# A two-layer S5/FNet backbone in split fp32r: seams between sections run in two halves of the tokens, with three PSUM slots

## What is computed

```python
def _pre(x, g, mod, k):
    return _rmsnorm(x, g) * (1.0 + mod[:, 3 * k + 1][:, None]) + mod[:, 3 * k][:, None]
def _post(x, y, g, mod, k, weight):
    return x + weight * mod[:, 3 * k + 2][:, None] * _rmsnorm(y, g)
...
for l in range(DEPTH):
    x = _post(x, _swiglu(_pre(x, g[0], mod_lat, 0), ffn1_gu[l], ffn1_down[l]), g[1], mod_lat, 0, 0.5)
    h = _pre(x, g[2], mod_lat, 1) @ w_in[l]
    y = jnp.concatenate([_s5_mixer(...), _fnet(...)], axis=-1) @ w_out[l]
    x = _post(x, y, g[3], mod_lat, 1, 1.0)
    x = _post(x, _swiglu(_pre(x, g[4], mod_lat, 2), ffn2_gu[l], ffn2_down[l]), g[5], mod_lat, 2, 0.5)
```

## Time and profile before

| what | us |
|---|---|
| runs of the program: median (lowest to highest) | 2869.12 (2868.15 to 2871.7) |
| the profiled execution: its time | 2866.32 |
| the profiled execution: its span in the trace | 2864.4 |
| PE busy | 2680.7 (94%) |
| DVE busy | 1677.3 (59%) |
| POOL busy | 821.0 (29%) |
| ACT busy | 716.3 (25%) |

### The profile page before, as it was taken

The page is one execution under the profiler, slowest core; times in us unless marked ns, Lnnn a source line. Parts: engine busy times, 40 slices in busy tenths (PEclk is TensorE's granted clock), DMA queues, the critical chain, the costliest instruction groups (busy, mean ns, idle before and its releaser), DMA issues.

```text
span 2864.4 us, 39514 instructions
## 1 busy us (share of the span) xinstructions
PE 2680.7 (94%) x16446; PEld 2496.0 (87%) x16446; DVE 1677.3 (59%) x2235; ACT 716.3 (25%) x977; POOL 821.0 (29%) x1292
## 2 busy tenths in 40 slices
PE   5899999998899889999999799999998898899996
PEld 4899999997869789999999699999998766588885
DVE  5868877865582686766665743343434683644444
ACT  4211121113413421111111322112122413322222
POOL 1258775732050200000000228767551050100001
PEclk9999999999999999999999899999999999899998
DMA  9443444442455134343441232222233455133321
GB/s 314 125 132 125 152 152 128 129 165 87 151 147 162 45 111 125 111 130 114 132 126 52 74 74 87 95 94 89 94 103 120 138 167 161 57 96 99 96 89 59
DMA packets 340459, 337.09 MB, mean 118 GB/s; under 512 B 52529, under 2 KB 311225, under 8 KB 336697
## 3 DMA queue, kind: packets, MB, share of 16 engines
q1 hardware_dynamic: 279224, 204.07, 24.3%
q10 hardware_dynamic: 51840, 77.07, 8.0%
q0 software_dynamic: 9216, 53.42, 5.0%
...
...
## 4 chain that ended last, share of the span: by engine, by line
PE 81%; DVE 11%; ACT 3%; DMA 2%; issue 2%; SPq 1%; POOL 0%; DVEq 0%; ACTq 0%; POOLq 0%
PE ps L454 71%; DVE adaW L541 3%; PE ps L1390 2%; PE ps L582 2%; PE ps L1089 2%; ACT wH L439 1%; PE ps L1415 1%; DVE tmpN L1168 1%; DMA y_d<-YC 1%; DVE wL L446 1%; DVE rmsX L1177 1%; DVE xT L1049 1%; PE ps L1404 1%; DMA xin<-in_x_dram 1%; PE ps L1074 1%
## 5 line engine op out<-in xcount | busy, mean ns | idle before, releaser
L454 PE MATMUL ps<-hH,wH 128*128 128x384 f32 (+1 forms) x2928 | 1019.9, 348 | 67.9 <-DVE hL L1186 48.1
L454 PE MATMUL ps<-hL,wH 128*128 128x384 f32 (+1 forms) x2928 | 1011.6, 345 | 0.0
L454 PE MATMUL ps<-hH,wL 128*128 128x384 f32 (+1 forms) x2928 | 1010.9, 345 | 0.0
L446 DVE TENSOR_TENSOR wL<-raw,wH 128x1024 fp32r<-128x1024 f32 x300 | 392.0, 1319 | 551.9 <-ACT wH L439 551.3
L454 PEld LDWEIGHTS ps<-hH,wH 128*128 128x128 f32 x2928 | 556.1, 190 | 95.6 <-issue 55.9
L454 PEld LDWEIGHTS ps<-hL,wH 128*128 128x128 f32 x2928 | 556.3, 190 | 18.1
L454 PEld LDWEIGHTS ps<-hH,wL 128*128 128x128 f32 x2928 | 555.5, 190 | 18.5
L454 PE MATMUL ps<-midH,wH 128*128 128x384 f32 (+1 forms) x1232 | 426.2, 346 | 12.7 <-DVE wL L446 9.9
L454 PE MATMUL ps<-midH,wL 128*128 128x384 f32 (+1 forms) x1232 | 423.6, 344 | 0.0
L454 PE MATMUL ps<-midL,wH 128*128 128x384 f32 (+1 forms) x1232 | 423.2, 344 | 0.0
L439 ACT ACTIVATE wH<-raw 128x1024 fp32r<-128x1024 f32 x300 | 310.8, 1050 | 448.2 <-PE ps L454 399.3
...
## 6 DMA issues: line engine op xcount, KB each, us to landing
...
```

The costliest lines, as they stand in the source:

```text
L446: nc.vector.tensor_tensor(wL[:, n % SPLIT_SLOTS, :], raw[:, n % RAW_SLOTS, :], wH[:, n % SPLIT_SLOTS, :].bitcast(f32), ALU.subtract).then_ ...
L454: ins = nc.tensor.matmul(dst, a, b, start=first and n == 0, stop=last and n == 3 * len(pairs) - 1)
```

## The change

**Halves.** `part(tok0, h)` is half h of the tokens: 384 and 384, or 256 and 256 of the latent ones. The last down pass becomes `last_down`: all 8 tiles for half 0, then all 8 for half 1, each 6 matmuls of 384 columns (of 256, in F2_1). In a mixer state tiles 0 and 1 stay whole, 2 to 7 run by halves. Each half has its own squares, sums, root, reciprocal and spread, in banks 6 and 7. PE does half 0's y_stat behind tile 2 of half 1 (3 in a mixer) and its y_spread behind tile 4.

**The second norm.** x is normalised as y was: POOL sums six squares, DVE adds the last, PE does small statistics by blocks of 128 tokens and a spread. The full-width matmuls of L1089, the wide root and the wide reciprocal of L1177 are gone, but for the program's start. All additions to x are on DVE. The `late` units are split after x's second half. In `first_groups` the halves are the outer loop; half 1's x_stat and x_spread stand at k = 2 and k = 4 of half 0. ACT takes half 1's root before it shifts chunk 2 of half 0.

**Slots.** `F.slots` is 3 in every FFN, `OUT_SLOTS` has three entries, which keeps banks 6 and 7 free.

**Rides.** A ride's matmuls stand before the up tile, its copy and the next DMA issue before midH. The first two pieces are issued at the program's start, the first 16 steps stand behind the up tiles' work on DVE.

**Others.** SP loads the Fourier weights before the last down units; the matmuls of the head weights stand ahead of the last down pass and their copy (CW) behind it, no longer in the mixer; the end's transposes start with the first half's tokens.

The diff, cut to what the prediction speaks of:

```diff
-        F.slots = 3 if gen else 4
+        F.slots = 3
...
+    def part(tok0, h):
+        w = (TOK - tok0) // 2
+        return tok0 + h * w, w
...
     def first_groups(pe, base, count, pre):
 
-        pe.wait_ge(w_lo, base + count)
-        for k in range(KC):
-            pe.wait_ge(h_lo, KC * pre.nth + k + 1)
-            for u in range(count):
-                wh, wl = wtile(base + u)
-                for i, (t0, w) in enumerate(halves(pre.tok0)):
+        for u in range(count):
+            pe.wait_ge(w_lo, base + u + 1)
+        for h in range(2):
+            t0, w = part(pre.tok0, h)
+            for k in range(KC):
+                if pre.after and h == 0 and k == 2:
+                    x_stat(pe, pre, 1)
+                if pre.after and h == 0 and k == 4:
+                    x_spread(pe, pre, 1)
+                pe.wait_ge(h_lo, 2 * KC * pre.nth + h * KC + k + 1)
+                for u in range(count):
+                    wh, wl = wtile(base + u)
+                    dst = ps[:, 2 * u, t0 - CTX:t0 - CTX + w] if pre.tok0 else ps[:, 2 * u + h, 0:w]
                     ins = three([(wh[:, k, :], wl[:, k, :], hH[:, k, t0:t0 + w], hL[:, k, t0:t0 + w])],
-                                ps[:, 2 * u + i, 0:w], k == 0, k == KC - 1)
-                if k == KC - 1:
-                    ins.then_inc(w_used, 1)
+                                dst, k == 0, k == KC - 1)
+                    if h == 1 and k == KC - 1:
+                        ins.then_inc(w_used, 1)
...
-                ride = F.ride0 + 2 * s + i // 2 if F.ride0 is not None and i % 2 == 0 else None
+                ride = F.ride0 + 2 * s + i // 2 if F.ride0 is not None and i % 2 else None
...
+    def last_down(pe, F):
+        n = F.base + 6 * NPH - 2
+        pe.wait_ge(w_lo, n + 2)
+        pe.wait_ge(mid_lo, F.n0["mid_lo"] + FC)
+        (ah, al), (bh, bl) = wtile(n), wtile(n + 1)
+        s0 = (FC - 2) % 4
+        for h in range(2):
+            for m in range(KC):
+                if m >= F.slots:
+                    pe.wait_ge(last_read, F.n0["last_read"] + KC * h + m - F.slots + 1)
+                elif h == 0:
+                    wait_tile(pe, F, LAST_TILE + m - F.slots)
+                at = cols(F.tok0, h)
+                ins = three([(ah[:, m, :], al[:, m, :], midH[:, s0, at], midL[:, s0, at]),
+                             (bh[:, m, :], bl[:, m, :], midH[:, s0 + 1, at], midL[:, s0 + 1, at])],
+                            last_tile(F, h, m), True, True)
+                if h == 0 or m < KC - 1:
+                    ins.then_inc(last_ps, 1)
+                else:
+                    ins.then_inc(w_used, 2)
+                if h == 1 and m == 2:
+                    y_stat(pe, F.post, F, 0)
+                if h == 1 and m == 4:
+                    y_spread(pe, F.post, 0)
...
-            if ride is not None:
-                take_columns(act, ride, 2 * tile_slot(F, g), TOK // 2)
-                next_ride(ride + 2)
...
+            if ride is not None:
+                take_columns(act, ride, 2 * tile_slot(F, g), TOK // 2)
+                next_ride(ride + 2)
...
-    POOL_CHUNKS = (1, 3, 5)
-    DVE_CHUNKS = tuple(m for m in range(KC) if m not in POOL_CHUNKS)
...
+    def norms_pool(pool, N, nxt):
+        for h in range(2):
+            add_squares(pool, N, h, sq_y, sumY, sum_y)
+        if nxt:
+            for h in range(2):
+                add_squares(pool, N, h, sq_x, sumX, sum_x)
...
+    def norms_tensor(pe, N, S, nxt):
+        y_stat(pe, N, S, 1)
+        y_spread(pe, N, 1)
+        if nxt:
+            x_stat(pe, nxt, 0)
+            x_spread(pe, nxt, 0)
...
+        root(act, N, 0, X_COL, ss_x, sd_x)
         for m in range(KC):
...
+            square_x(act, N, 1, m)
+        for m in range(2):
+            add_shift(act, nxt, 0, m)
+        root(act, N, 1, X_COL, ss_x, sd_x)
+        for m in range(2, 2 * KC):
+            add_shift(act, nxt, m // KC, m % KC)
...
+        for m in range(m0, KC):
+            take(dve, S, 0, m)
+        last_squares(dve, N, 0, sq_y, sumY, sum_y, all_y)
+        for m in range(m0, KC):
+            take(dve, S, 1, m)
+            if not ffn and m in (3, 5):
+                split_lo(dve, S.base + 18 + m // 4)
+            if m == (2 if ffn else 3):
+                invert(dve, N, 0, sd_y, rs_y)
+            if m == 4:
+                wait_back(dve, N)
+            if 4 <= m < 7:
+                new_x(dve, N, 0, m - 4)
+        last_squares(dve, N, 1, sq_y, sumY, sum_y, all_y)
+        for m in range(3, KC):
+            new_x(dve, N, 0, m)
+            if m == 5:
+                invert(dve, N, 1, sd_y, rs_y)
+        for m in range(KC):
+            new_x(dve, N, 1, m)
+            if nxt and m == 3:
+                last_squares(dve, N, 0, sq_x, sumX, sum_x, all_x)
+            if nxt and m == 6:
+                invert(dve, N, 0, sd_x, rs_x)
+        if not nxt:
+            return
         for n in S.late:
             split_lo(dve, n)
...
+        def source(h, t0, t1):
+            return spread_ps(nxt.tok0, h, t0, t1)
         dsync(dve)
...
+        for i in range(2 * KC):
+            h, m = divmod(i, KC)
+            if m == 0:
+                dve.wait_ge(bc_x, nth_of(N, h) + 1)
+            scale_h(dve, nxt, h, m, source)
+            if i:
+                rest_h(dve, nxt, (i - 1) // KC, (i - 1) % KC)
+            if i == 1:
+                last_squares(dve, N, 1, sq_x, sumX, sum_x, all_x)
+            if i == 3:
+                invert(dve, N, 1, sd_x, rs_x)
+        rest_h(dve, nxt, 1, KC - 1)
...
-    OUT_SLOTS = (2, 0, 1, 3)
+    OUT_SLOTS = (2, 0, 1)
...
+        for m in range(2):
+            state_whole(m)
+        for h in range(2):
+            for m in range(2, KC):
+                state_part(h, m)
+                if h and m == 3:
+                    y_stat(pe, M.post, M, 0)
+                if h and m == 4:
+                    y_spread(pe, M.post, 0)
```

484 lines of the change are left out of this document (287 added, 197 removed).

## The result

The changed kernel takes 2884.36 us (median of 6 runs, 2878.63 to 2886.71), the kernel before 2868.64 in the same comparison (6 runs, 2864.69 to 2871.70). The ratio is 1.0054, 95% interval 1.0041 to 1.0067: slower by .54%. The prediction was 2877 with a range of 2850 to 2897, and .48 on slower. So 8 us more were forecast than the kernel before took, and 15.7 more were measured. The profiled execution of the changed kernel took 2882.29 us with a span of 2880.5, 16.1 more than before.

The account below looks back on a forecast made before the run. PE, busy 94% of the span, was taken as the bound, so its stands count. Terms 1.2 + 4.8 - 1.5 - 6.0 - 9.4 made 10.9 us more, 2880 for the median, less 3: 2877, range 2850 to 2897.

Parts of the forecast that it names:

- Third slot in F2_1: F2_1 down passes: tile 3 waits for DVE's read of tile 0, .9 us a pass, 9.4 us lost over ten.
- Third slot and ride copy in F2_0: F2_0 passes: tile 3 waits and the ride's copy delays midH; .7 us a pass, nine passes, 6.0 us lost.
- The seams: Six stretches from a last projection to the next section's first units: overlapping halves gain 1.2 us in sum.
- the wait of additions to x for POOL: In the seams, each DVE addition meeting a POOL sum waits in full; without POOL waits about +30 instead of +1.2 us.
- the fourth rival: Matmuls of 256 columns start .174 us apart, not .123: 20 us more, 2895; chance .16 together with The third, the clock.
- F1_0: F1_0's rides: matmuls one tile later end PE's waits for ride steps and the half clock behind; 4.8 us gained.
- M1: Mixer M1: with three output slots the fifth fourier tile waits for ACT's read, runs cold, delays the first gate; 1.5 us lost.
- First, the halves pay: Seams: additions to x find POOL idle or wait little, +29 us over all, time 2851; chance .24.
- The second: F2_1 and F2_0: the added wait at tile 3 hides, 15 us of loss go, 2862 to 2865; chance .12.
- The third, the clock: Twenty passes' new waits each drop the clock, adding 20 to 26 us, 2897 to 2903; .16 with the fourth rival.
- The last 3 us of the sum: Whole program: 3 us taken off because the seam schedule lets every addition meeting POOL wait in full; 2880 becomes 2877.

Follow-up runs that it names:

- b_three_slots: Kernel before with only F2_0 and F2_1 cut from four PSUM slots to three; 2881.75 us, ratio 1.0039 to the kernel before.
- a_four_slots: Changed kernel with four slots again in F2_0 and F2_1 up to the last down pass; 2864.61 us, .9987 of the kernel before.
- c_unit_by_unit: As a_four_slots, with half 1's last two k of the first units done unit by unit; ratio .9985 to the kernel before.
- a_no_x_sums: Changed kernel with POOL adding one square of x per half instead of six; one profiled run, span 2863.4 us.

## Why the prediction was right, step by step

**Third slot in F2_1: right.** Put at .9 a pass and 9.4 us for ten (ten times .9 is 9.0); the matmul is .94 late and the pass 1.08 longer, 10.8 in all. It was read from three rows, and b_three_slots and a_four_slots show it alone and undone. What the step missed is the slow start behind the wait.

**Third slot and ride copy in F2_0: right in the pass, short in the sum.** .7 a pass was put, .88 measured, .44 for the slot and .43 for the copy, of which the copy was exact. The section lost 12.7 us and not 6.0: the passes make 8.0, and 4.7 stand at its start: 1.1 more ahead of the fourth unit (2.15 us for 1.03), .5 more ahead of the first ride (1.01 for .53), and 1.56 of half clock behind each, where there was none. That the halves free the first unit's weights later was not among my steps; it is the change to `first_groups` that I called harmless by not pricing it. The same term is the 2.5 us of F1_1 and .7 of F2_1's 11.5 (2.27 us for 1.54), and c_unit_by_unit shows the cause: freed earlier, the wait falls to 1.11.

**The seams: sign right, size too small.** I put +1.2 us for the six; measured 9.8, of which 4.5 is the clock at the start of three of them, which my schedule had left out of both kernels. That leaves 5.3 to compare with 1.2. By seam, put and measured: .3 and 1.6, -2.1 and 0.0, 2.7 and 4.8, .3 and 2.5, -3.8 and -4.3, 3.8 and 5.2. The step that was mis-sized is the wait of additions to x for POOL. I let each addition wait, 4.7 us in the seam of F2_0 and F1_1, and the splits 1.3 more; the rows show that mostly POOL waits, and a_no_x_sums puts what the sums left out cost there at 3.3. The first unit's start, 46.9 after the last projection's, came at 45.93. The stand of 1.9 us for half 1's root was 1.82, and the 3.1 us ahead of y_spread in M0 was 2.3. Matmuls of 256 columns, which no row had shown, start .12 apart, some 320 of 384 (I had .123; the others are at half clock or behind a wait), so the fourth rival is out.

**F1_0: wrong.** I put a gain of 4.8 us (its terms, 3.9 + 4.2 - 3.4 + .3, make 5.0), and it lost 5.8. The failed step is "the matmuls now stand one tile later, so this goes". The wait went; the next thing late was the piece of w_ada, which DVE waits for ahead of a split that PE needs. I had counted of the moved step its copy and its issue on ACT's queue, and not its landing. The experiment shows the two places of the ride to be equal within 2 to 3 us in F1_0. So of the 10.6 us by which this term is off, 4.8 are the gain that never was and 2.2 lie in the passes, within what a repeat differs by. The other 3.6 stand ahead of the first down pass (153.78 instead of 150.20): the first unit starts 1.4 us later, and the fourth unit's wait is 2.15 us here too. With the rides back the first down pass starts at 154.85 and 154.43, so this part is not theirs. Why the first unit is later was not tried.

**M1: the mechanism right, the sign wrong.** The fifth fourier tile waits for ACT's read, as predicted:

```profile
2407.12 0.79 PE L480 MATMUL ps<-hH,wH 128*128 128x512 f32 x1 [8.95 <-ACT yT L1854]
...
2411.60 0.40 PE L480 MATMUL ps<-hH,wH 128*128 128x512 f32 x1
```

But it starts before the gate's h is there, and with it PE spends its half-clock matmuls on a tile that would have come anyway. The gate itself, at 2411.60, then runs at full clock; in the earlier trace rows it was the gate that started cold, 2.2 us of half clock. The tile holds the gate back by .7 us (DVE's h for it is ready at 2410.89), so about 1.5 is won. M1 up to state tile 2 took 4.4 us less, 2.4 of it because the gate's weights landed 135.7 us after the section's start and not 138.0, behind a store of y that took 12.67 us instead of 13.98. Whether that store is faster by the change was not tried. M0's 2.2 us less, for which the prediction put nothing, was not traced either.

**The rivals.** First, the halves pay: in part. The seams gave 9.8 us and not 30; POOL's sums do cost 3.3 in the seam where it was counted, and 15.0 over the five. The second fell with the first row of F2_1. The third, the clock, fell too. The stretch of F2_1 with its ten waits of .78, granted clock in the third column from the end:

```profile
2500.55:2843.44 342.89, 335.07 (x1464) 273.89 (x1464) 153.95 (x184) 85.23 (x104) 0.00 (x0) 1.00 0.30 92
```

The waits of .58 in F2_0 left it up too. What was followed by half clock, in two FFNs of four, is the wait of about 2.15 us for the fourth unit, a kind I had not listed. The prediction's sentence that no row shows the clock falling for a wait below 1 us is not right, though: in F1_0 of the kernel before, the ride wait of .59 us at 581.39 was followed by matmuls .32 us apart from 583.49 on.

The Trainium skill ("SBUF — State Buffer", Who interferes with whom) says that issue order, and not the kind of instruction, decides which of the two engines blocks. The seam's rows agree. POOL's sum and a DVE addition that both start at 1613.63 take 1.40 and .55 us, so POOL waits; DVE's last sum of y, issued .31 us behind POOL's first sum of x, takes 1.10, and POOL's stays at .99.

That the sum came within .3% of the time owes something to luck, and the difference to the kernel before, put at 8 us, was 15.7. F1_0 was 10.6 us too good, F2_0, F1_1 and F2_1 together 11.3 too good, and against it the seams were 8.6 and the mixers 8.1 too bad, 3.0 of the former by a clock that fell in one trace and not in the other behind the same waits. The last 3 us of the sum, taken off since POOL's waits were counted in full, had the right reason and moved it away from the time.
